# Two-block mixture-of-experts kernel: gate and up pieces of the last two experts ahead of their down pieces, split buffers released singly, router tile by tile

## What is computed

```
t = moba_attention(h, a_w_in, a_w_out, rel_bias)            # 8 heads of 128, causal, 256 tokens
h = layer_norm(ALPHA * h + t, ln_g[0], ln_b[0])
logits = h @ w_router + b_router                            # 32 experts
top_logit, top_e = top_k(logits, 4); gate = softmax(top_logit)
for each expert e, on the tokens that chose it:
    gate_h, up_h = split(x_e @ w_gu[e] + b_gu[e])           # 1024 -> 2 * 1024
    act = min(gate_h, 7) * sigmoid(1.702 * min(gate_h, 7)) * (clip(up_h, -7, 7) + 1)
    f += gate * (act @ w_down[e] + b_down[e])               # 1024 -> 1024
h = layer_norm(ALPHA * h + f, ln_g[1], ln_b[1])
second_block(h)                                             # weights w_in_2, w_out_2, ffn_w_up_2, ffn_w_down_2
```

## Time and profile before

| what | us |
|---|---|
| median of 3 runs | 1436.23 |
| lowest and highest of them | 1432.08, 1436.34 |
| the profiled execution, its own time | 1436.48 |
| its span (first to last instruction) | 1434.7 |
| TensorE busy in the span | 1357.1 |
| VectorE, ScalarE, GpSimd busy | 438.8, 332.7, 41.8 |
| moved by DMA over the span | 483.12 MB, mean 337 GB/s |

### The profile page before, as it was taken

How to read it: one execution, slowest core, us unless ns; L and a number is a source line. 1 busy time by engine, 2 the same in 40 slices (tenths; PEclk the granted TensorE clock), 3 DMA queues, 4 the chain that set the end, 5 groups by cost and what they waited for, 6 DMA issues and landing times.

```text
span 1434.7 us, 16969 instructions
## 1 busy us (share of the span) xinstructions
PE 1357.1 (95%) x7356; PEld 725.3 (51%) x7356; DVE 438.8 (31%) x726; ACT 332.7 (23%) x543; POOL 41.8 (3%) x50
## 2 busy tenths in 40 slices
PE   7998999999869999999999999999989878999997
PEld 6996333333223333333333333333339875799986
DVE  4554211001011011011011000110048465588863
ACT  4440101101001011011001100111036422566642
POOL 1001000000000000000000000000000000022200
PEclk9998999999979999999999999999999999999999
DMA  9647899999999999999999999999985400645530
GB/s 378 272 191 282 364 431 431 430 430 431 431 414 428 430 431 430 430 430 431 430 431 431 430 431 431 430 430 431 431 328 191 176 30 1 235 178 184 193 122 30
DMA packets 44026, 483.12 MB, mean 337 GB/s; under 512 B 4684, under 2 KB 4736, under 8 KB 13360
## 3 DMA queue, kind: packets, MB, share of 16 engines
q1 hardware_dynamic: 42112, 476.58, 79.7%
q0 software_dynamic: 1840, 5.44, 1.1%
HBM read 480.94 MB, written 1.06 MB: 336 GB/s over the span
## 4 chain that ended last, share of the span: by engine, by line
PE 81%; DMA 11%; DVE 4%; issue 2%; ACT 1%; SPq 0%; DVEq 0%; ACTq 0%
PE bank L739 25%; PE bank L569 18%; PE bank L747 14%; DMA ring<-in_moe_w_gate_up 11%; PE bank L1004 4%; PE bank L759 3%; PE bank L712 3%; PE bank L551 3%; PE bank L731 2%; PE bank L964 2%; PE bank L658 2%; PE bank L682 1%; PE bank L925 1%; ACT w_hi L1057 1%; DMA ring<-in_a_w_in 1%
## 5 line engine op out<-in xcount | busy, mean ns | idle before, releaser
L739 PE MATMUL bank<-ring,arena 128*64 128x512 f32 x2048 | 452.3, 597 | 13.7 <-DMA ring<-in_moe_w_gate_up 13.7
L739 PEld LDWEIGHTS bank<-ring,arena 128*64 128x64 f32 x2048 | 143.3, 137 | 321.3 <-issue 290.0
L747 PE MATMUL bank<-ring,arena 128*64 128x512 f32 x1024 | 226.8, 595 | 0.9 <-ACT arena L1159 0.9
L1541 DVE TENSOR_SCALAR arena<-bank 128x512 f32<-128x512 f32 x32 | 22.1, 691 | 669.5 <-PE bank L739 669.4
L569 PE MATMUL bank<-x_hi,w_hi 128*128 128x256 f32 x640 | 185.2, 289 | 12.2 <-DVE w_lo L1354 10.1
L569 PE MATMUL bank<-x_lo,w_hi 128*128 128x256 f32 x640 | 182.8, 286 | 0.0
L569 PE MATMUL bank<-x_hi,w_lo 128*128 128x256 f32 x640 | 182.7, 285 | 0.0
L1340 DVE TENSOR_TENSOR w_lo<-ring,w_hi 128x2048 fp32r<-128x2048 f32 x61 | 139.6, 2291 | 123.2 <-ACT w_hi L1057 123.2
L1057 ACT CAST w_hi<-ring 128x2048 fp32r<-128x2048 f32 x61 | 116.4, 1908 | 113.2 <-PE bank L569 87.5
L747 PEld LDWEIGHTS bank<-ring,arena 128*64 128x64 f32 x1024 | 70.7, 137 | 135.7 <-issue 127.9
L1153 ACT ACTIVATE arena<-arena 128x512 f32<-128x512 f32 x32 | 20.2, 630 | 502.6 <-DVE arena L1541 502.6
(11 more groups left out here) (270 smaller groups left out, 1123.6 us busy)
## 6 DMA issues: line engine op xcount, KB each, us to landing
ring<-in_moe_w_gate_up SPq DMA_DIRECT2D x128, 2048.0 KB, 25.3
ring<-in_moe_w_down SPq DMA_DIRECT2D x64, 2048.0 KB, 27.2
ring<-in_ffn_w_up SPq DMA_DIRECT2D x22, 1024.0 KB, 4.8
ring<-in_w_in SPq DMA_DIRECT2D x14, 1024.0 KB, 6.2
ring<-in_a_w_in SPq DMA_DIRECT2D x11, 1024.0 KB, 19.0
ring<-in_ffn_w_down SPq DMA_DIRECT2D x11, 1024.0 KB, 4.8
ring<-in_a_w_out SPq DMA_DIRECT2D x2, 2048.0 KB, 20.7
ring<-in_w_out SPq DMA_DIRECT2D x2, 2048.0 KB, 8.3
```

Source lines behind the costliest of these rows:

```text
L739: last = mm(bank[q // 2][half * 64:half * 64 + 64, :], chunk(xeT, c), w[:, c % 2, q * 512:(q + 1) * 512], start=False, stop=c == KC - 1)
L747: last = mm(bank[3][half * 64:half * 64 + 64, :], chunk(actT, c), w[:, c % 4, half * 512:(half + 1) * 512], start=c == 0, stop=c == KC - 1)
```

## The change

The order of loads and products becomes a list, `piece_order`: experts 0 to 29 as before, then the gate and up pieces of experts 30 and 31, then the down pieces of 30, then those of 31. The four buffers that the output projection uses are given back one after the other. `w_hi` and `w_lo` are interleaved, so that each of places 6 to 8 holds one weight part. The layer norm and the router choice work half by half and tile by tile, two repeats become single ones at other places, five repeats of zeros stand at the start, and tables are loaded and used later.

```diff
+        w_split = sb("w_split", [P, SPLITS, 2, HALF], SPLIT_FIRST * SLOT, f32r)
+        w_hi, w_lo = w_split[:, :, 0, :], w_split[:, :, 1, :]
+        OUT_ORDER = (3, 0, 1, 2)
+        GATE_UP, LAST = 4, N_EXP - 1
+        piece_order = [(i, s) for i in range(LAST - 1) for s in range(PIECES_E)]
+        for part in (range(GATE_UP), range(GATE_UP, PIECES_E)):
+            piece_order += [(i, s) for i in (LAST - 1, LAST) for s in part]
...
             for p in range(1, 8):
                 sp.dma_start(a_place(p), a_w_in[p, :, :]).then_inc(attn_w[p % 8], 16)
-                if p == 1:
+                if p == 2:
                     sp.dma_start(cst[:, :], consts[:, :]).then_inc(rest_in, 16)
...
-            sp.wait_ge(out_ps, NT)
-            load_piece(SPLIT_X)
-            for n in range(SPLIT_FIRST, SPLIT_LAST + 1):
-                load_piece(n)
+            for k, q in enumerate(OUT_ORDER):
+                sp.wait_ge(*((out_used, k + 1) if k < PAIRS - 1 else (out_ps, NT + 1)))
+                load_piece(SPLIT_X if q == SPLITS else SPLIT_FIRST + (OUT1 + q) % SPLITS)
...
+            pool.memset(at(2048, 512), 0.0).then_inc(zeros_ready, 1)
+            pool.wait_ge(first_in, 16)
             pool.dma_start(bucket_sb, buckets[:, :]).then_inc(rel_in, 16)
...
+            pool.wait_ge(attn_w[0], 16)
             fc = ffn_conv.rearrange("j (f p) -> (j f) p", p=P)
...
+            pe.wait_ge(zeros_ready, 1)
+            repeat(0, 5, at(2048, P), at(2048, 512))
...
                     if half:
                         last.then_inc(proj_ps, 1)
-                    elif r == 0:
-                        pe.wait_ge(rel_in, 48)
-                        mm(bank[7][0:H, :], relb_sb, bucket_sb, start=True, stop=True).then_inc(rel_ps, 1)
-                    elif r == 1:
+                        if r == 0:
+                            pe.wait_ge(rel_in, 48)
+                            mm(bank[7][0:H, :], relb_sb, bucket_sb, start=True, stop=True).then_inc(rel_ps, 1)
+                    elif r == 2:
...
-            for q in range(PAIRS - 1):
-                out_part(q, 1)
-            out_part(PAIRS - 1, 1).then_inc(out_ps, 1)
+            for g in range(2):
+                for q in OUT_ORDER:
+                    last = out_part(q, 1, (g,), OUT_ORDER[0], OUT_ORDER[-1])
+                    if g and q != OUT_ORDER[-1]:
+                        last.then_inc(out_used, 1)
+                last.then_inc(out_ps, 1)
...
+                if i == LAST:
+                    put_down(LAST - 1)
+                elif i and i != EXTRA_AFTER + 1:
...
-                turn_chunks(3, act_e.rearrange("p c n -> p (c n)"), 4).then_inc(actT_ps, 1)
+                turn_chunks(2 if i == LAST else 3, act_e.rearrange("p c n -> p (c n)"), 4).then_inc(actT_ps, 1)
+                if i == LAST:
+                    pe.wait_ge(y_ready, LAST)
+                    for t in range(NT):
+                        scatter(t)
...
                 elif IN2 <= p < IN2 + SPLITS:
-                    act.wait_ge(piece_done, place_free(SPLIT_LAST))
+                    act.wait_ge(piece_done, place_free(SPLIT_FIRST + p % SPLITS))
...
-            for b in (4, 6):
+            for b in (4, 5, 6):
...
-            dve.wait_ge(rel_ps, 1)
-            tt(rel_tab, bank[7][0:H, :], behind_sb, ALU.add).then_inc(rel_ready, 1)
-            split_lo(IN1 + 1)
+            split_lo(IN1 + 1)
+            dve.wait_ge(rel_ps, 1)
+            tt(rel_tab, bank[7][0:H, :], behind_sb, ALU.add).then_inc(rel_ready, 1)
...
-            link(stt(place.rearrange("p t e -> p (t e)"), bank[0][:, 0:2 * N_EXP], FAR,
-                     chosen.rearrange("p t e -> p (t e)"), ALU.add, ALU.mult))
-            ts(place, place, -FAR, None, ALU.add).then_inc(place_ready, 1)
+            stt(place.rearrange("p t e -> p (t e)"), bank[0][:, 0:2 * N_EXP], 0.5,
+                chosen.rearrange("p t e -> p (t e)"), ALU.add, ALU.mult).then_inc(place_ready, 1)
```

More of the change, by code:

```diff
@@ L571, in product, with repeat @@
                     yield last
+            def repeat(b, n, a=None, v=None):
+                for _ in range(n):
+                    mm(bank[b][:, :], ident if a is None else a, cst[:, 0:512] if v is None else v, start=True, stop=True)
+            pe.wait_ge(zeros_ready, 1)
+            repeat(0, 5, at(2048, P), at(2048, 512))
             pe.wait_ge(xT_hi, 1)
@@ L641, in _, with out_part @@
                         scores(2 * j + 1)
-                    elif part == 0:
+                    elif part == 0 and j:
                         turn_probs(2 * j - 2)
                         turn_probs(2 * j - 1)
-                    elif part == 1:
+                    elif part == 1 and j:
                         pe.wait_ge(proj_act, 2 * j)
                         values(j - 1)
-            def out_part(q, t):
+            def out_part(q, t, halves=(0, 1), first=0, last_q=PAIRS - 1):
                 pe.wait_ge(lo_ready, OUT1 + q + 1)
@@ L654, in out_part @@
                     a_hi, a_lo = (v[:, h, t * P:(t + 1) * P] for v in (o_hi, o_lo))
-                    for g in range(2):
+                    for g in halves:
                         cols = slice(g * 512, (g + 1) * 512)
                         for k, (a, w) in enumerate(((a_hi, hi), (a_hi, lo), (a_lo, hi))):
-                            last = mm(bank[OUT_BANKS[2 * g + t]][:, :], a, w[:, cols], start=h == 0 and k == 0,
-                                      stop=h == H - 1 and k == 2)
+                            last = mm(bank[OUT_BANKS[2 * g + t]][:, :], a, w[:, cols], start=h == 2 * first and k == 0,
+                                      stop=h == 2 * last_q + 1 and k == 2)
                 return last
@@ L674, in _ @@
             pe.wait_ge(exp_ready, H)
-            for q in range(PAIRS - 1):
-                out_part(q, 1)
-            out_part(PAIRS - 1, 1).then_inc(out_ps, 1)
-            def repeat(b, n):
-                for _ in range(n):
-                    mm(bank[b][:, :], ident, cst[:, 0:512], start=True, stop=True)
+            for g in range(2):
[4 more added lines that the diff above has]
+                last.then_inc(out_ps, 1)
+            before = const("before")
             for t in range(NT):
@@ L774, in _, with put_down @@
             turn_chunks(2, xe, 2).then_inc(xeT_ps, 1)
+            def put_down(i):
+                pe.wait_ge(actT_ready, i + 1)
+                for s in range(2):
+                    n = piece_at[i, GATE_UP + s]
+                    pe.wait_ge(ring_in[n % SLOTS], 16 * (n // SLOTS + 1))
+                    down_e(s, slot(n % SLOTS, 4)).then_inc(piece_done, 1)
             for i in range(N_EXP):
@@ L781, in _ @@
                 pe.wait_ge(xeT_ready, i + 1)
-                for s in range(4):
-                    n = PIECES_E * i + s
+                for s in range(GATE_UP):
+                    n = piece_at[i, s]
                     pe.wait_ge(ring_in[n % SLOTS], 16 * (n // SLOTS + 1))
@@ L1399, in _ @@
                 split_lo(r + SPLITS)
+                if r == 1:
+                    dve.wait_ge(vcol_ps, 1)
+                    dve.tensor_copy(vcol[:, :], bank[7][:, 0:164]).then_inc(vcol_ready, 1)
                 if r == 2 or part == 1 and j:
```

111 lines of the change are left out of this document (53 added, 58 removed).

## The result

| | before | changed kernel |
|---|---|---|
| median, us (6 runs each) | 1435.7 | 1426.11 |
| lowest to highest, us | 1431.28 to 1437.21 | 1423.73 to 1429.99 |
| profiled execution: its time, span | 1436.48, 1434.7 | 1425.4, 1423.6 |

The ratio is 0.9945, with a 95% interval of 0.9927 to 0.9963: 9.6 us faster by the medians, 7.9 by the ratio, inside the range and 0.6 under the forecast. The profiled execution of the changed kernel lies 0.7 under its median and that of the kernel before 0.8 above its own, so single landmarks (the times at which named steps start or end) say more than the totals. Counted from the start of the span, the output projection ends 2.21 earlier (121.73), the first gate and up piece starts 9.40 earlier (138.60), the last down piece ends 10.85 earlier (1045.78) and the first product of the second block starts 10.84 earlier (1067.43).

The account below looks back on a forecast made before the run. The prediction took the stream of expert pieces to bound the expert stage, so its start counted. Start 2.3, output projection and router 6.3, last two experts 1.2: 9.8 off 1436.48 gives 1426.7 us; 8-in-10 range 1423 to 1431.

Parts of the forecast that it names:

- Start: Up to the output projection: earlier low part, repeats of zeros and later tables and constants win 2.3 us.
- At most 1 us later: At the start: the relative table is ready at most 1 us later than before, so the bias should not delay TensorE.
- Router: Output projection and router: fewer waits and reordered TensorE work bring the gather earlier, worth 6.3 us, bounds 3 and 7.1.
- The steps of 7.05: Router steps timed from the projection's end at full clock: gather at + 12.5 instead of + 19.56, 7.05 us won.
- T0: End of the output projection: 124.12 us in the kernel before, expected near 121.8 in the changed one.
- Rival 1: Router: the clock stays low through most of it, leaving 3 of the 6.3, total near 6.8, 1429.7 us; chance 0.16.
- The stream: Loads of expert pieces: they keep up with the earlier router, so its whole 6.3 us goes through.
- the ring: The places that hold loaded pieces: expected full 20.1 us behind the output projection's end, ahead of the first use.
- the hole: Pause in transfers before the first gate and up piece is used: TensorE, not the loads, still ends it.
- joint release: Output projection's four buffers given back together: caps the router's gain at 4.2 us, so single release is worth 2.1.
- Tail: Last two experts: the new piece order ends the last down product 4.1 us behind the last landing, not 5.3; worth 1.2.
- At nothing: Parts priced at zero, including the second block's high part waiting for its own place, up to 2 us if ScalarE's order allowed.

Follow-up runs that it names:

- e7: Changed kernel with GpSimd's tables loaded at once and the constants loaded behind part 1 again; median 1428.59 us, ratio 0.9944.
- e2: Changed kernel without the five repeats of zeros at the start; median 1426.75 us, ratio 0.9937.
- e5: Kernel before with only the half by half output projection of tile 1, interleaved split buffers and singly released places added; median 1436.29 us, ratio 0.9995.
- e8: Kernel before without its two pairs of repeats in the router; median 1438.08 us, ratio 1.0017.
- e4: Changed kernel without its four single repeats in the router; median 1432.25 us, ratio 0.9981.
- e3: Changed kernel with the output projection's four buffers released together at its end; median 1428.16 us, ratio 0.9948.
- e1: Changed kernel with the old order of pieces and down products for the last two experts; median 1427.07 us, ratio 0.9946.
- e6: Changed kernel with VectorE's low part of the second block's first weight part moved behind the second norm's last scaling; median 1425.03 us, ratio 0.993.

## Why the prediction was right

**Start, 2.3: measured 2.21, in part by luck.** The sum held, its parts were mis-sized. Later tables and constants were to give 0.3; e7 says 0.8. The zeros give 0.7 (e2). The remaining 0.7 can't be put down to the low part standing ahead of the table. TensorE ran at half its rate until 16.9 us before, but only until some 14 us in e5 and e8, which have the same start; there r = 1 starts at 19.0 and 19.29 instead of 19.89, and the projection ends at 123.07 and 123.34 instead of 123.94. So 0.6 to 0.9 of the 2.21 is what the one execution before lost there, and against e5 and e8 the new start gives 1.3 to 1.6. No experiment undid the order of the low part alone. "At most 1 us later" held for the relative table (0.8), but its rows took 5.66 through DRAM where they took 4.45, so that the bias transfer was issued 2.0 later; it cost nothing, since the transfer landed within the 7.7 us between its issue and the scores.

**Router, 6.3: measured 7.19 to the first gate and up piece,** and 6.08 against e5, whose router is the same as before and had the full clock in its second pair of repeats. The 6.3 lies between, so its size is as good as these executions can tell. The steps of 7.05 came out at T0 + 12.55 for a predicted 12.5, and the steps before it came within 0.3 of theirs; the 0.75 charged for one stretch at the lower clock was not spent in the profiled execution. e2 and e7 show that such a stretch costs 0.6 to 0.7 where it does come, in three of ten profiles, so the size was about right and its presence is chance. Rival 1, that the clock stays low, was a fair description of e4: what decides it are the four repeats. Its price held too: it left 3.3 of the router and 6.8 in all, and e4 has 3.4 at the first piece and 6.7 at the end of the experts, though its median lies only 3.5 under that of the kernel before, since the second block took longer in it (359.29 in its profile against 356.43). The rule on short idle spells, from the Trainium skill's page "TensorE: Matmul & The Clock Gate", section "A second HAM failure mode: psum-queue depth-cycling", was weighed in the prediction. The trace of e4 agrees with it, where gaps of 0.72 to 1.52 us went with a granted clock of 0.50; in the changed kernel, with a repeat at four places, gaps of 0.28 to 0.73 did not bring the clock down, and in three of the ten profiles of that order a stretch of it still came.

**The stream, the whole 6.3 going through.** Transfers resume at 118.5, 3.2 ahead of T0 where 3.2 were worked out (4.1 less 0.9), and the ring is full at 142.0 = T0 + 20.3 for a predicted 20.1. TensorE ends the hole, 1.0 us long. The price of a joint release was put at 2.1 and measured at 1.7 (e3).

**Tail, 1.2: measured 1.45 in the changed kernel and 1.49 against e1.** The last product ends 4.0 behind the last landing for a predicted 4.1.

**At nothing.** The high part of the second block's first weight part moved nothing: 21.65 from the last down piece to the product in both kernels. The prediction saw "up to 2 us" there if ScalarE's order let it through; e6 found 3.4 in the same stretch from VectorE's order, which the prediction did not look at.

The sum of the measured terms is 2.21 + 7.19 + 1.45 = 10.85, one more than the 9.8 of the prediction, and that is what the profiled execution shows; the medians differ by 9.6. Against e5, in which single release gave nothing, the experts end 8.97 earlier. The forecast lies between the two. That it met the medians' difference to 0.2 is luck at this size: two profiles with the same start and router differ by 1.9 us at the end of the experts, and more profiles of either kernel, which would settle it, were not taken.

## What to carry to other kernels

When a stream of loads must start late, look at both of its ends: what frees the first places, and what first uses them. Here the earlier release alone gave nothing to the stream and only made the hole ahead of the first use longer, and the earlier first use alone left 1.7 us behind. Repeats of a constant product between short dependent products are not idle work: taking them away cost 5 to 6 us in one kernel and 2.3 in the other. And where executions of one kernel spread over 6 us, find the stretch whose clock differs before measuring effects of 1 us by medians, and don't take one profile of either side for the kernel.

## What the hardware showed that I had not expected

- The granted clock of one stretch (60 to 90 us into the second block) read 0.73 to 1.00 in different executions of the same instructions. In e1's profile it was 1.00 without any added repeat, and the second block took 353.05 us, the least of all; at 0.73 to 0.98 it took 356.17 to 359.34. With ten repeats there the spread of 6 us between executions fell to 1.9.
- TensorE's rate at the start does not show in the granted clock: it read 1.00 while matmuls ran 0.21 us apart. In e2, e5 and e8 they came to 0.12 at 13.5 to 14.3 us, before only at 16.9.
- A GpSimd subtraction over 128x2048 took 4.52 us, about twice VectorE's 2.29, and made a one-column VectorE operation last 3.25 us instead of 0.21.
